# Merge gates of a hybrid decoder layer as seven block products each

## The chip, the cores and the metric

The kernel runs on one core of a Trainium2 chip. TensorE multiplies matrices into PSUM (8 banks of 128 x 512 fp32), VectorE, ScalarE and GpSimd work element by element, and DMA queues that SyncE issues move data between DRAM and SBUF. Each engine runs its own instructions strictly in the order in which they are written and meets the others through semaphores. The metric is the device time of one execution in microseconds. Every matrix product has fp32 accuracy by three passes: each operand is split into hi (ScalarE, a rounding copy) and lo (VectorE, the difference), and TensorE adds hi x hi, hi x lo and lo x hi.

## What is computed

One decoder layer: a half-step FFN, a token mixer with two branches, a half-step FFN. The part that matters here is the mixer, cut from the reference (1024 positions, model width 1024):

```python
u = _rmsnorm(h, mix_pre_g[l])
c_q, c_kv, k_rope_raw, xb, yb, gate_mla, gate_lru = jnp.split(u @ w_in[l], split_points, axis=-1)
o_mla = _mla_branch(c_q, c_kv, k_rope_raw, positions, ...)   # norms, up-projections, rotary, causal softmax, output projection
o_lru = _rglru_branch(xb, yb, conv_w[l], ...)                # below
merged = jax.nn.sigmoid(gate_mla) * o_mla + jax.nn.sigmoid(gate_lru) * o_lru
h = h + _rmsnorm(merged @ w_out[l], mix_post_g[l])

# _rglru_branch
xc = conv_b + sum(xpad[:, k:k + s] * conv_w[k] for k in range(CONV_WIDTH))
r  = jax.nn.sigmoid(einsum('bsgi,gij->bsgj', xg, w_rg) + b_rg)     # xg: xc in 8 blocks of 128
ig = jax.nn.sigmoid(einsum('bsgi,gij->bsgj', xg, w_ig) + b_ig)
a = jnp.exp(log_a);  gated_x = jnp.sqrt(-jnp.expm1(2.0 * log_a)) * (ig * xc)
_, h = lax.associative_scan(_lru_combine, (a, gated_x), axis=1)
return (h * jax.nn.gelu(yb)) @ w_o_lru
```

## The kernel before

Activations lie transposed, channels on partitions: `u_hi` and `u_lo` hold u as 8 chunks of 128 channels by 1024 positions. A projection of 128 output channels by all positions is 8 chunks x 2 halves x 3 passes = 48 matmuls of 512 columns. Weights come as blocks of 512 KB into a raw ring of three slots (`w.load` on SyncE, which waits until the block three before it is split); `w.hi` on ScalarE and `w.lo` on VectorE split them into a ring of three. The order of every engine's work is written out by hand.

The recurrence runs over 8 columns d of 128 channels. In round d TensorE does `gates_of(d)` (12 matmuls, recurrence and input gates from the convolved column), `y_of(d+1)` (48) and `x_of(d+2)` (48). VectorE convolves column d+1 out of PSUM (one tensor-scalar, three dependent multiply-adds), splits it, forms the factor under the root (`mix`), runs the scan (`scan`) and multiplies by the gelu branch (`gated`); between these it does the weight lo parts. ScalarE does the two sigmoids, the hi parts, two exponentials and a tanh (`decay`), the square root (`root`) and the next gelu; each change of function set is a table load. GpSimd multiplies twice per column (`products`). The finished column is split (`out_hi`, `out_lo`) into `lru_hi`, `lru_lo` in SBUF, where the branch projection reads it.

Then comes `LruMerge`: for each d, 48 matmuls of the gate (`gate_of`), whose sigmoid ScalarE takes out of PSUM, and 48 of the projection by w_o_lru (`branch_of`); VectorE multiplies both and the product goes to DRAM (`mixed_scratch`). After it `Latents`: eight tiles of 128 positions, `project` (48 matmuls of 384 or 288 columns), squares, scaling and transposes (`turn`), with one gate of the attention branch (`gate_of`, 48 matmuls) ahead of all but two of the projections, two of them ahead of the first; their sigmoids go to DRAM. Last, the value products (`v_of`) and the first units (`unit_of`) of attention, then the softmax steps; GpSimd clears six half-empty operand tiles (`blank`) before the first of them and divides each step's probabilities.

The two FFNs already use the block scheme that the change brings to the gates: a product of two 2 x 2 block matrices in seven block products instead of eight, with sums of blocks formed beforehand.

## Time and profile before

| | us |
|---|---|
| median of 3 runs | 2288.66 (2287.89 to 2289.98) |
| the profiled execution's own time | 2287.68 |
| its span, first to last instruction | 2285.9 |
| TensorE busy | 2154.8 (94%), 9837 matmuls |
| VectorE busy | 1387.9 (61%) |
| ScalarE busy | 975.1 (43%) |
| GpSimd busy | 450.0 (20%) |
| mean granted TensorE clock | 0.979 of full |

The span is cut by the profile into starts and durations of every instruction, in microseconds from its start. The listed duration of a matmul includes its way through the array; neighbours overlap, so what one costs is the distance between starts. The recurrence's rounds lie at 742 to 906, the gates and branch projection of `LruMerge` from there to 1080, the latents to 1231, attention's softmax steps from 1253 on.

### The profile page before, as it was taken

How to read it: one execution, taken by the hardware profiler on the slowest of the kernel's cores; microseconds unless marked ns; L12 is line 12 of the kernel's file. 1: busy time of each engine (PE TensorE's matmuls, PEld its weight loads, DVE VectorE, ACT ScalarE, POOL GpSimd, SP SyncE). 2: the span in 40 equal slices, each digit the busy share in tenths (PEclk: the TensorE clock that was granted, in tenths of full speed). 3: DMA queues.
4: the chain of work that ended last, by engine and by line, in shares of the span. 5: the costliest groups of instructions: out<-in, count | busy, mean ns of one | idle time of the engine just before them, and what ended most of it. 6: DMA issues, size and time to landing. Idle time of an engine off the chain costs nothing.

```text
span 2285.9 us, 25908 instructions
## 1 busy us (share of the span) xinstructions
PE 2154.8 (94%) x9837; PEld 1788.0 (78%) x9837; DVE 1387.9 (61%) x1718; ACT 975.1 (43%) x1543; POOL 450.0 (20%) x453
## 2 busy tenths in 40 slices
PE   4999999999998999999999888998599999999997
PEld 3888788878886888888888777777488888888885
DVE  7668865557575656211213788677756766557666
ACT  5333333334353776311323666445433333334343
POOL 5123320000032221000012555215312321000012
PEclk8999999999999999999999999999799999999998
DMA  3345442252442221222410100455135453216334
GB/s 120 93 155 187 155 168 69 70 198 96 154 148 78 52 52 49 74 65 77 119 43 23 29 15 10 161 194 175 55 96 188 168 192 124 72 51 221 101 134 143
DMA packets 220294, 249.85 MB, mean 109 GB/s; under 512 B 24262, under 2 KB 161547, under 8 KB 220171
## 3 DMA queue, kind: packets, MB, share of 16 engines
q1 hardware_dynamic: 220170, 248.19, 33.3%
q8 instruction: 79, 1.29, 0.2%
q14 instruction: 45, 0.36, 0.1%
HBM read 192.06 MB, written 55.57 MB: 108 GB/s over the span
## 4 chain that ended last, share of the span: by engine, by line
PE 86%; DVE 6%; ACT 3%; POOL 3%; issue 2%; DMA 1%; POOLq 0%; SPq 0%; ACTq 0%; DVEq 0%
PE ps L88 28%; PE ps L90 28%; PE ps L89 28%; PE ps L2172 1%; PE ps L2140 1%; POOL a_rot L2057 1%; PE ps L357 1%; ACT a_probs L2116 1%; DVE a_pt L98 1%; DVE ff_t L98 1%; DVE a_s L2106 0%; DVE entry_y L342 0%; DVE w_lo L98 0%; DMA w_raw<-in_w_out_dram 0%; ACT entry_squares L282 0%
## 5 line engine op out<-in xcount | busy, mean ns | idle before, releaser
L98 DVE TENSOR_TENSOR ff_w_lo<-ff_raw,ff_w_hi 128x512 fp32r<-128x512 f32 x264 | 210.9, 802 | 171.9 <-ACT ff_w_hi L94 171.7
L88 PE MATMUL ps<-ff_t,ff_w_hi 128*128 128x512 f32 x704 | 275.5, 391 | 15.8 <-DVE ff_t L98 15.8
L89 PE MATMUL ps<-ff_t,ff_w_hi 128*128 128x512 f32 x704 | 275.1, 391 | 0.0
L90 PE MATMUL ps<-ff_t,ff_w_lo 128*128 128x512 f32 x704 | 275.1, 391 | 0.0
L94 ACT ACTIVATE ff_w_hi<-ff_raw 128x512 fp32r<-128x512 f32 x264 | 164.8, 628 | 180.4 <-PE ps L90 174.9
L88 PE MATMUL ps<-d_b_hi,d_a_hi 128*128 128x512 f32 x608 | 237.6, 391 | 3.7 <-DVE d_a_lo L98 3.7
L98 DVE TENSOR_TENSOR w_lo<-w_raw,w_hi 128x1024 fp32r<-128x1024 f32 (+2 forms) x81 | 93.6, 1160 | 237.4 <-ACT w_hi L94 237.3
L90 PE MATMUL ps<-d_b_hi,d_a_lo 128*128 128x512 f32 x608 | 236.8, 390 | 0.0
L89 PE MATMUL ps<-d_b_lo,d_a_hi 128*128 128x512 f32 x608 | 236.8, 389 | 0.0
L88 PE MATMUL ps<-ff_b,ff_w_hi 128*128 128x512 f32 x528 | 209.0, 396 | 13.5 <-issue 8.3
L89 PE MATMUL ps<-ff_b,ff_w_hi 128*128 128x512 f32 x528 | 207.8, 394 | 0.0
L90 PE MATMUL ps<-ff_b,ff_w_lo 128*128 128x512 f32 x528 | 207.6, 393 | 0.0
L88 PE MATMUL ps<-u_hi,w_hi 128*128 128x512 f32 x512 | 201.0, 393 | 2.4 <-DVE u_lo L98 2.4
L89 PE MATMUL ps<-u_lo,w_hi 128*128 128x512 f32 x512 | 200.4, 391 | 0.0
L90 PE MATMUL ps<-u_hi,w_lo 128*128 128x512 f32 x512 | 200.4, 391 | 0.0
L88 PEld LDWEIGHTS ps<-ff_t,ff_w_hi 128*128 128x128 f32 x704 | 133.0, 189 | 44.0 <-issue 16.3
L89 PEld LDWEIGHTS ps<-ff_t,ff_w_hi 128*128 128x128 f32 x704 | 132.9, 189 | 27.6
L90 PEld LDWEIGHTS ps<-ff_t,ff_w_lo 128*128 128x128 f32 x704 | 132.8, 189 | 27.7
L94 ACT ACTIVATE w_hi<-w_raw 128x1024 fp32r<-128x1024 f32 (+2 forms) x81 | 78.1, 968 | 165.2 <-PE ps L90 155.0
L88 PEld LDWEIGHTS ps<-d_b_hi,d_a_hi 128*128 128x128 f32 x608 | 114.2, 188 | 28.9 <-DVE d_a_lo L98 5.7
L90 PEld LDWEIGHTS ps<-d_b_hi,d_a_lo 128*128 128x128 f32 x608 | 114.2, 188 | 23.8
L89 PEld LDWEIGHTS ps<-d_b_lo,d_a_hi 128*128 128x128 f32 x608 | 114.2, 188 | 23.5
(296 smaller groups left out, 4362.4 us busy)
## 6 DMA issues: line engine op xcount, KB each, us to landing
ff_raw<-in_ffn_w_gate_dram SPq DMA_DIRECT2D x44, 512.0 KB, 3.9
ff_raw<-in_ffn_w_up_dram SPq DMA_DIRECT2D x44, 512.0 KB, 4.0
d_sums<-in_ffn_w_down_dram SPq DMA_DIRECT2D x44, 512.0 KB, 4.1
sums_scratch<-d_sums SPq DMA_DIRECT2D x88, 256.0 KB, 2.6
w_raw<-in_w_in_dram SPq DMA_DIRECT2D x32, 512.0 KB, 3.9
d_raw<-sums_scratch SPq DMA_DIRECT2D x24, 512.0 KB, 3.3
w_raw<-in_w_out_dram SPq DMA_DIRECT2D x24, 512.0 KB, 4.3
spill_scratch<-ff_st SPq DMA_DIRECT2D x44, 256.0 KB, 2.6
```

The costliest lines, as they stand in the source:

```text
L88: pe.matmul(out, lh, rh, start=start, stop=False, skip_group_check=go_on)
L89: pe.matmul(out, lh, rl, start=False, stop=False, skip_group_check=go_on)
L90: return pe.matmul(out, ll, rh, start=False, stop=stop, skip_group_check=go_on)
L94: return nc.scalar.activation(hi, src, ACT.Copy)
L98: return nc.vector.tensor_tensor(lo, src, as_f32(hi), ALU.subtract)
L357: last = pe.transpose(self.c.ps[:, b + k // 4, (k % 4) * P:(k % 4 + 1) * P], self.work(t)[:, k * P:(k + 1) * P], self.c.ident[:, :])
L2057: self.nc.gpsimd.tensor_tensor(self.rot[rope, :], self.rot[rope, :], self.rot2[rope, :], ALU.add)\
L2116: self.nc.scalar.activation(self.prob(n), self.seen(n), ACT.Exp, bias=self.neg[:, i:i + 1], scale=1.0, accum_out=self.rs[:, i:i + 1]).then ...
L2140: last = pe.transpose(c.ps[:, 4 + b, at * P:(at + 1) * P], self.prob(n)[:, j * P:(j + 1) * P], c.ident[:, :])
L2172: last = pe.matmul(c.ps[:, 6, first * P:HALF], self.v[:, h, j, :], pt[:, unit, first:4, :].rearrange("p b q -> p (b q)"), start=j + i == 0 ...
```

## The change

Both gates are taken out of `LruMerge` and `Latents` and computed together by a new class, `MergeGates`, right after the recurrence. For each gate, w_gate^T u is a product of 2 x 2 blocks (halves of the channels, halves of the positions and of the inputs). A chunk m is one pair of 128-channel rows, one in each half; there are 8 chunks, 4 for each gate, and for each of them seven products p of 12 matmuls, 672 in all where there were 768. The sums of activation blocks (`t_wholes`, `t_sums`, `t_hi`, `t_lo`) are formed once, during the recurrence's rounds 1 to 5, the last one at its end; the sums of weight blocks (`sums`) per chunk. Three PSUM banks serve a chunk, and a product that continues in a bank waits until ScalarE has copied out the bank's state (`snap`); VectorE adds further banks (`cadd`) into the copy.

The space that `lru_hi` and `lru_lo` had holds the activation sums now. So a recurrence column is stored to DRAM unsplit (`keep`), and the next convolution into its buffer waits for that store. The columns are loaded and split again after the last latent projection (`row_hi`, `row_lo`) into the place of u, and the branch projection stands there, behind the latents; the gates' sigmoids all go to DRAM and those of this branch are loaded back for its products. The last column's projection is cut into its lo half and two hi halves, with the first attention units between them. The clearing of attention's tiles waits until the last product is stored.

The diff, cut:

```diff
+def gate_order():
+
+    order = [(0, 1), (0, 2), (0, 6), (0, 7), (0, 5)]
+    for m in range(1, G_CHUNKS):
+        order += [(m, 1), (m, 2), (m - 1, 3), (m - 1, 4), (m, 6), (m, 7), (m, 5)]
+    return order + [(G_CHUNKS - 1, 3), (G_CHUNKS - 1, 4)]
...
+    def product(self, pe, m, p):
+        c, F, S = self.c, self.c.f, self.rec.S
+        self.wait_split(pe, m, p)
+        if p == 1:
...
+            elif m == 0:
+                pe.wait_ge(S["conv_done"], DK)
+                pe.wait_ge(S["gelu_done"], DK)
...
+        if p == 6:
+            pe.wait_ge(F.snap[1], self.nm(m))
...
+        if p == 5:
+            pe.wait_ge(F.snap[6], self.nm(m))
...
+        for k in range(4):
+            lhs = tuple(x[:, slot, k * P:(k + 1) * P] for x in (self.hi_at, self.lo_at))
+            last = mm3(pe, out, lhs, self.right_of(p, k), k == 0 and p in (1, 2, 7), k == 3, p not in (1, 2, 7))
...
-    def out_hi(self, act, d):
...
+    def keep(self, sp, d):
+
+        sp.wait_ge(self.S["out_done"], d + 1)
+        sp.dma_start(self.kept[d * P:(d + 1) * P, :], self.xc[:, d % 2, :]).then_inc(self.c.f.d_in[2 + d % 2], 16)
...
     def convolve(self, dve, d):
         self.w.wait_done(dve, self.n_x[d])
         if d >= 2:
-            dve.wait_ge(self.S["out_split"], d - 1)
+            self.wait_kept(dve, d - 2)
...
     def blank(self, pool):
-        pool.wait_ge(self.lat.S["proj_done"], NT)
+        self.wait_unit(pool, self.units[0])
+        self.merge.all_stored(pool)
...
                     rec.mix(dve, d)
                     rec.scan(dve, d)
-                    if d + 2 <= DK:
-                        w.lo(dve, (rec.n_y + [ring[1]])[d + 2])
+                    if 1 <= d <= 4:
+                        gates.t_sums(dve, d - 1)
+                    if d + 2 < DK:
+                        w.lo(dve, rec.n_y[d + 2])
                     rec.gated(dve, d)
...
-                lru.gate_of(pe, 0)
-                lru.gate_of(pe, 1)
-                lru.branch_of(pe, 0, tuple(range(DK - 1)))
-                lru.branch_of(pe, 0, (DK - 1,))
...
+                for m, p in G_ORDER:
+                    gates.product(pe, m, p)
                 lat.project(pe, 0)
-                lat.project(pe, 1)
-                lat.turn(pe, 0)
-                for s in range(2, NT):
-                    lat.gate_of(pe, s)
+                for s in range(1, NT):
+                    lat.project(pe, s)
                     lat.turn(pe, s - 1)
-                    lat.project(pe, s)
-
-                att.v_of(pe, 0)
-                att.v_of(pe, 1)
+
+                for t in range(4):
+                    att.v_of(pe, t)
+                lat.turn(pe, NT - 1)
+                for k in range(DK):
+                    for d in range(2):
+                        lru.branch_of(pe, d, k)
+                    if k < 4:
+                        att.v_of(pe, k + 4)
+                for d in range(2, DK - 1):
+                    for k in range(DK):
+                        lru.branch_of(pe, d, k)
+                lru.last_lows(pe)
                 att.unit_of(pe, units[0])
...
+                lru.last_highs(pe, 0)
                 att.unit_of(pe, units[2])
-                att.v_of(pe, NT - 1)
+                lru.last_highs(pe, 1)
                 att.unit_of(pe, units[3])
```

What stands in a row on three engines, before and after. VectorE in a middle round of the recurrence, before, from the scan to the next convolution:

```order
L1499 SCALAR_TENSOR_TENSOR r_xc<-r_a,r_xc 128x1024 [waits r_bx_done]
L98 TENSOR_TENSOR w_lo<-w_raw,w_hi 128x1024 [waits w_hi_done]
L1505 TENSOR_TENSOR r_xc<-r_xc,r_gate_y_140 128x1024 [waits r_gelu_done,r_scan_done]
L98 TENSOR_TENSOR lru_lo<-r_xc,lru_hi 128x1024 [waits r_out_hi]
L98 TENSOR_TENSOR w_lo<-w_raw,w_hi 128x1024 [waits w_hi_done]
L1478 TENSOR_SCALAR r_xc<-ps,params 128x1024 [waits r_out_split,w_used]
```

After, from the scan of round 3 to the next convolution (`g_t_raw` is the activation sums' raw place, `g_t` their hi and lo parts):

```order
L1502 SCALAR_TENSOR_TENSOR r_xc<-r_a,r_xc 128x1024 [waits r_bx_done]
L1657 TENSOR_TENSOR g_t_raw<-g_t_raw 128x512 [waits g_t_sum]
L1658 TENSOR_TENSOR g_t_raw<-g_t_raw 128x512
L1660 TENSOR_TENSOR g_t_raw<-g_t_raw 128x512 [waits g_t_sum]
L1663 TENSOR_TENSOR g_t_raw<-g_t_raw 128x512 [waits g_t_sum]
L98 TENSOR_TENSOR w_lo<-w_raw,w_hi 128x1024 [waits w_hi_done]
L1508 TENSOR_TENSOR r_xc<-r_xc,r_gate_y_140 128x1024 [waits r_gelu_done,r_scan_done]
L98 TENSOR_TENSOR w_lo<-w_raw,w_hi 128x1024 [waits w_hi_done]
L98 TENSOR_TENSOR g_t<-g_t_raw,g_t 128x4x512 [waits g_t_hi]
L1641 TENSOR_TENSOR g_t_raw<-u_hi,u_lo 128x2x512
L1644 TENSOR_TENSOR g_t_raw<-u_hi,u_lo 128x2x512
L1481 TENSOR_SCALAR r_xc<-ps,params 128x1024 [waits d_in2,w_used]
```

The split of the finished column went out; four sums came between scan and weight split, and the split of an earlier set and two adds of whole operands between the last weight split and the convolution, which now waits for the store (`d_in2`).

ScalarE at the end of the recurrence (last column), before, from the first exponential to the first gate's sigmoid:

```order
L1452 ACTIVATE r_a<-r_r,rates 128x1024 [waits r_sig_r]
L1454 ACTIVATE r_b<-r_r,rates 128x1024 [waits r_ix_done]
L1457 ACTIVATE r_r<-r_r,rates 128x1024 [waits r_a2_done,r_a_done]
L1461 ACT_TABLE_LOAD
L1461 ACTIVATE r_r<-r_r 128x1024 [waits r_m_done]
L94 ACTIVATE lru_hi<-r_xc 128x1024 [waits r_out_done]
L94 ACTIVATE w_hi<-w_raw 128x1024 [waits w_used,w_raw_in1]
L1602 ACT_TABLE_LOAD [waits r_out_split]
L1602 ACTIVATE m_sig_149<-ps 128x1024 [waits w_used]
```

After, the same place (`g_w_hi` is the operand ring of the gates, `g_sig` the copies of banks):

```order
L1451 ACTIVATE r_a<-r_r,rates 128x1024 [waits r_sig_r]
L1453 ACTIVATE r_b<-r_r,rates 128x1024 [waits r_ix_done]
L1456 ACTIVATE r_r<-r_r,rates 128x1024 [waits r_a2_done,r_a_done]
L1460 ACT_TABLE_LOAD
L1460 ACTIVATE r_r<-r_r 128x1024 [waits r_m_done]
L1778 ACTIVATE g_sig_153<-ps 128x512 [waits r_out_done,f_prod]
L94 ACTIVATE g_w_hi<-g_s_151 128x512 [waits f_prod,f_sums]
L94 ACTIVATE g_w_hi<-w_raw 128x512 [waits f_prod,f_raw_in2]
L1796 ACT_TABLE_LOAD
L1796 ACTIVATE g_sig_153<-g_sig_153 128x512 [waits f_cadd2]
L1778 ACTIVATE g_sig_154<-ps 128x512 [waits f_prod]
```

Behind the root there now stands the copy of the first product's bank; the first sigmoid of a gate and the copy of the third product's bank follow it.

GpSimd at attention's start, before:

```order
L1967 MEMSET a_q_167 32x1024 [waits l_proj_done]
L1967 MEMSET a_q_169 32x1024
L1967 MEMSET a_k_171 32x1024
L1967 MEMSET a_k_174 32x1024
L1967 MEMSET a_k_172 32x1024
L1967 MEMSET a_k_175 32x1024
L2057 TENSOR_TENSOR a_rot<-a_rot,a_rot_178 32x512 [waits a_q_rot,a_zero]
L1752 TENSOR_TENSOR l_kr_t<-l_kr_t,trig 32x512 [waits l_c_split,l_rs_done,a_q_sum]
L1755 TENSOR_TENSOR l_rot<-l_rot,l_kr_t 32x512 [waits l_swapped,l_plain]
L2057 TENSOR_TENSOR a_rot<-a_rot,a_rot_178 32x512 [waits a_q_rot,l_rotated]
L2122 TENSOR_TENSOR a_s_184<-a_s_183,expo 128x1 [waits a_p_done,a_q_sum]
L2125 TENSOR_SCALAR a_probs<-a_probs,a_s_184 128x128 [waits a_norm_done]
```

After:

```order
L2375 TENSOR_TENSOR a_rot<-a_rot,a_rot_185 32x512 [waits a_q_rot,l_rotated]
L2375 TENSOR_TENSOR a_rot<-a_rot,a_rot_185 32x512 [waits a_q_rot,a_q_sum]
L2287 MEMSET a_q_174 32x1024 [waits m_stored0,m_stored1,a_unit_done,a_q_sum]
L2287 MEMSET a_q_176 32x1024
L2287 MEMSET a_k_178 32x1024
L2287 MEMSET a_k_181 32x1024
L2287 MEMSET a_k_179 32x1024
L2287 MEMSET a_k_182 32x1024
L2440 TENSOR_TENSOR a_s_191<-a_s_190,expo 128x1 [waits a_p_done,a_zero]
L2443 TENSOR_SCALAR a_probs<-a_probs,a_s_191 128x128 [waits a_norm_done]
```

The six clearings went behind the rotary sums and wait for the stores of the mixed products (`m_stored`) and the first unit; the first division of probabilities follows them as before.

## Rows read from the trace of the kernel before

**Rows 1.** Page, parts 1 and 4: busy time, and the chain that ended last.

```profile
PE 2154.8 (94%) x9837; PEld 1788.0 (78%) x9837; DVE 1387.9 (61%) x1718; ACT 975.1 (43%) x1543; POOL 450.0 (20%) x453
...
PE 86%; DVE 6%; ACT 3%; POOL 3%; issue 2%; DMA 1%; POOLq 0%; SPq 0%; ACTq 0%; DVEq 0%
```

**Rows 2.** Busy time by stretch.

```profile
core 0: us, PE busy (x) PEld busy (x) DVE busy (x) ACT busy (x) POOL busy (x), PEclk, DMA share, GB/s
735.00:906.00 171.00, 171.00 (x756) 141.69 (x755) 107.69 (x85) 121.74 (x115) 33.65 (x14) 1.00 0.19 48
1096.00:1231.00 135.00, 135.00 (x740) 122.23 (x739) 22.40 (x52) 39.71 (x115) 12.70 (x30) 1.00 0.21 59
1231.00:1260.00 29.00, 23.38 (x108) 18.18 (x106) 19.49 (x34) 17.31 (x39) 12.34 (x15) 1.00 0.04 9
```

**Rows 3.** TensorE timeline: start, duration, both in us, then line, operands, shape.

```profile
889.58 0.39 PE L88 MATMUL ps<-r_xc_hi,r_g_hi 128*128 128x512 f32 x1
...
905.90 0.39 PE L88 MATMUL ps<-u_hi,w_hi 128*128 128x512 f32 x1
```

**Rows 4.** VectorE timeline, one round of the recurrence.

```profile
792.03 1.34 DVE L1478 TENSOR_SCALAR r_xc<-ps,params 128x1024 f32<-128x1024 f32 x1
...
797.24 1.22 DVE L98 TENSOR_TENSOR r_g_lo<-r_raw_g,r_g_hi 128x256 fp32r<-128x256 f32 x1
...
808.05 2.29 DVE L1499 TENSOR_TENSOR_SCAN r_xc<-r_a,r_xc 128x1024 f32<-128x1024 f32 x1 [3.62 <-POOL r_xc L1519]
...
813.72 1.23 DVE L98 TENSOR_TENSOR lru_lo<-r_xc,lru_hi 128x1024 fp32r<-128x1024 f32 x1 [1.13 <-ACT lru_hi L94]
...
816.34 1.34 DVE L1478 TENSOR_SCALAR r_xc<-ps,params 128x1024 f32<-128x1024 f32 x1 [0.26 <-PE ps L90]
```

**Rows 5.** GpSimd, ScalarE and VectorE timelines, and tile a_o_lo: durations.

```profile
795.77 2.41 POOL L1516 TENSOR_TENSOR r_xc<-r_b,r_xc 128x1024 f32<-128x1024 f32 x1 [11.72 <-ACT r_b L1444]
...
740.64 2.00 ACT L94 ACTIVATE w_hi<-w_raw 128x1024 fp32r<-128x1024 f32 x2
...
741.72 2.36 DVE L98 TENSOR_TENSOR w_lo<-w_raw,w_hi 128x1024 fp32r<-128x1024 f32 x2 [2.06 <-ACT w_hi L94]
...
L98 DVE TENSOR_TENSOR a_o_lo<-a_o,a_v x2: 683/688/693, 1453.9 to 1468.4; 128x512 fp32r<-128x512 f32 x2
```

**Rows 6.** ScalarE and VectorE timelines, end of the recurrence.

```profile
912.40 1.28 ACT L1444 ACT_TABLE_LOAD   x1
...
921.88 1.06 ACT L1461 ACTIVATE r_r<-r_r 128x1024 f32<-128x1024 f32 x1
...
925.44 2.29 DVE L1499 TENSOR_TENSOR_SCAN r_xc<-r_a,r_xc 128x1024 f32<-128x1024 f32 x1 [3.61 <-POOL r_xc L1519]
```

**Rows 7.** TensorE timeline after a long idle, and busy time of that stretch.

```profile
57.06 0.77 PE L88 MATMUL ps<-ff_t,ff_w_hi 128*128 128x512 f32 x1 [15.78 <-DVE ff_t L98]
...
57.00:62.30 5.30, 5.24 (x13) 4.14 (x14) 5.27 (x8) 0.88 (x2) 1.04 (x1) 0.51 0.00 0
```

**Rows 8.** ScalarE and VectorE timelines around the latent projections.

```profile
1080.17 2.08 ACT L94 ACTIVATE l_w_hi<-w_raw 128x672 fp32r<-128x672 f32 x3 [9.76 <-PE ps L90]
...
1093.99 0.86 DVE L98 TENSOR_TENSOR l_w_lo<-w_raw,l_w_hi 128x672 fp32r<-128x672 f32 x1 [1.37 <-ACT l_w_hi L94]
...
1234.27 0.94 ACT L1716 ACTIVATE l_lat<-ps,l_s 128x384 f32<-128x384 f32 x2 [0.82 <-POOL l_s L1740]
...
1244.38 0.88 ACT L1725 ACTIVATE cq<-ps,params 128x128 fp32r<-128x128 f32 x3
```

**Rows 9.** TensorE and GpSimd timelines at attention's start, and a DMA issue.

```profile
1253.62 0.33 PE L88 MATMUL ps<-a_k,a_q 96*128 96x128 f32 x1 [0.94 <-DVE a_v L98]
...
1260.63 0.48 PE L2140 MATMUL ps<-ident,a_probs 128*128 128x128 f32 x1 [0.31 <-POOL a_probs L2125]
...
1235.97 3.62 POOL L1967 MEMSET a_k<- 32x1024 f32 x4
...
mixed_scratch<-m_prod SPq DMA_DIRECT2D x8, 512.0 KB, 3.7
```

707 lines of the change are left out of this document (483 added, 224 removed).

## The prediction, made before the changed kernel was timed

> **What bounds the kernel now.** I read three views in this order. The page's busy line and its chain that ended last say TensorE: 2154.8 us busy of 2285.9, 86% of the chain [rows 1]. An average over stages does not say what an edit is worth, so next comes the busy time by stretch: from 735 to 906 (recurrence) and from 1096 to 1231 (latents) TensorE has no gap at all, and only around 1231 to 1260 (entry to attention) does it lose 5.6 us [rows 2]. So in the stretches that the change rewrites, TensorE's queue is the time. A matmul of 512 columns costs its issue pace, not its listed 0.39 us: 12 + 48 + 12 matmuls lie between 889.58 and 905.90, 0.227 us each [rows 3]. Last I read VectorE, ScalarE and GpSimd in one round of the recurrence [rows 4, 5]. They are not the bound, but their round is one chain: the next convolution starts 816.34 - 792.03 = 24.3 us after the last, against TensorE's round of 108 matmuls, 24.5 us, and two microseconds of that go to waits for each other. Whoever adds work in line there has almost no room.
>
> **What it removes.** Gates: 768 matmuls become 672. 96 x 0.227 = **-21.8 us**, on the path, since TensorE never waits there. Branch projection, latents and attention keep their matmul counts. The 16 weight splits, 16 gate sigmoids and the split of the recurrence's result come back as 56 splits, 32 half-wide sigmoids, 24 copies, 24 adds, 32 sums: per block row some 9 to 10 us of VectorE at 0.69 each [rows 5] beside 84 matmuls (19 us). From the second block row on that stays hidden: a copied bank is asked for two or more products later (5.4 us), and the operand ring is four products deep. I take 0 for the steady state, 0 to +4 for the range.
>
> **What it adds in the recurrence.** In rounds 1 to 4 VectorE gets two whole-operand adds, four sums and a split of 2048 columns, ScalarE a split of 2048. The order puts the sums between scan and weight split, the split and the adds before the next convolution: all of it in line, none of it in the gaps where VectorE waits for ScalarE and GpSimd. A round from convolution to convolution: to the scan's end 18.3 (792.03 to 810.34) [rows 4]; sums 4 x 0.65 = 2.6; ScalarE's split of the sums, which stands ahead of the next weight's hi part, 2.0, that hi part 1.0, the lo part 1.15; the split's lo part 2.3; the adds 2 x 1.15 = 2.3 (1024 columns pace 1.15 on VectorE, 1.0 on ScalarE) [rows 5]. Sum 29.7 against TensorE's 24.5. The pair of splits it saves (2.3 with its wait of 1.13) is already out of that sum. Starts: round 1 at 768.1 as before (what it gains, the first adds take); then 797.8, 827.5, 856.8 (the fourth set has one block less), 882.5 (only three sums, no further adds). Round 6 has only two half-wide splits, but its convolution now waits until the buffer it overwrites has been stored: gated product 1.2, then a store that lands in some 3.2 us (the same size took 3.7 on median [rows 9]; this buffer's twin in the latents stage was quicker). 906.4, where before stood 889.8: 16.6 late.
> TensorE absorbs part. Its round d needs the weight split that now stands behind the sums, and convolution d+1 before it may overwrite its bank; going through rounds 3 to 5 with these starts it waits 3.0, 4.8 and 2.5 us. Its last recurrence matmuls need the convolved column split at 906.4 + 7.7 = 914.1 and end at 916.8 instead of 905.9: **+10.9** (bounds 6 and 16).
> A rule that bears on this: the row of 797.24 shows a 256-column split on VectorE stretched to 1.22 us; it ended 0.28 us after GpSimd's product (795.77 + 2.41), while the convolution, which reads PSUM, ran through beside that product undisturbed [rows 4, 5]. The Trainium skill (SBUF — State Buffer, section SBUF: two separate sides) says that a VectorE instruction with two SBUF inputs and a GpSimd instruction that reads SBUF exclude each other for the whole instruction. The new adds and split have two SBUF inputs; by the rule they would sit out part of GpSimd's product. In the new round GpSimd's product would start about 26.3 us after the convolution (sums split 22.9, hi part 1.0, table load 1.3, sigmoid 1.1), just ahead of the adds at 27.4: up to 1.6 us more in each of three rounds. I count it as a rival.
>
> **What it does at the seam.** Before, 24 us of other matmuls (two gates, most of a projection) ran while the last column's sigmoids, exponentials, root and scan finished; ScalarE's root ended at 922.94, 17 us after TensorE was done with the recurrence, and nobody waited [rows 3, 6]. Now the first product waits for the last gelu, and the third waits for ScalarE's copy of the first one's bank, which stands behind that root. Counted from the last convolution's start C: scan 18.3, gated 1.2, four sums 2.7, two hi parts 1.2 on ScalarE, then table load to root 10.5 (912.40 to 922.94) [rows 6], copy 0.6: C + 34.5 = 940.9. Gelu: root 13.5, table load and gelu 2.4, so C + 15.9 = 922.3, **+5.5**. Two products take 5.4, then TensorE stands **13.2** us until 940.9. The fifth product waits for the copy of the third's bank, behind a sigmoid that waits for VectorE's add, which stands behind scan and gated product (2.4 + 2.3 + 1.2 + 0.7 + 0.6 + 0.6 after the root): **+2.0**. Seam: +20.7; even without any delay from the rounds it would be 12.8 + 2.0. After an idle of 15.78 us the granted clock read 0.51, its 1.2 GHz level, for 5.2 us, so 12 matmuls took 0.43 us each, 2.4 more in all [rows 7]; here the first ones after 940.9 would be as slow, and the wait of 2.0 swallows most: **+0.4** (0 to 5).
>
> **What it does in the latents and after.** No gates are left to lie between the projections. (a) The first projection wants eight split weights. The raw ring holds three; each later one costs a load of 3.5 us after a split, and the eight took from 1080.17 to 1094.85 [rows 8], hidden then by 21.8 us of gates. Now only two products (5.4 us) and the projection's own 7.6 cover them, and VectorE's last bank add stands among the splits: **+3.7** with the last chunk's exposed copy (2 to 7). (b) Behind the last projection ScalarE has some 7.5 us queued (squares, columns 1.5, scaling 0.94, two row copies of 1.0, two half-wide ones) [rows 5, 8] while TensorE has 4.8 of transposes and value products: **+3.3** (0 to 6). The rows read back from DRAM start three deep and are eaten at 2.7 to 4.1 us each: hidden. The five later projections, 10.9 us each, cover their weights and gate loads: 0. (c) Units of attention now alternate with the last column's halves, which covers TensorE's waits before 1253.62, some 3.4 of the 5.6: -3.4. But GpSimd's six clearings (5.4 us) [rows 9], before already begun at 1234, now wait until the last product has been stored, and the first softmax's division waits behind them: product 4.4 us after the last unit, store 3.7, clearings 5.5, against 6.3 us before: +7.4, of which short early steps catch up some 2. Net **+2** (-3 to +7).
>
> **Sum**, against the profiled execution's own 2287.7 (span 2285.9 plus 1.8 around it; the median is 2288.7): -21.8 + 10.9 + 20.7 + 0.4 + 3.7 + 3.3 + 2 = +19.2: **2307**.
>
> **Rivals.** (1) The shared port holds the adds back: three rounds of 1.6 more, 2312. For it, the 797.24 row; against, the late order may move GpSimd's product clear of them. (2) Slack absorbs the recurrence: if VectorE's new work costs nothing in line (its busy time would be only some 23 of 24.5 us), just the seam's 14.8 stays: -21.8 + 14.8 + 0.4 + 7 + 2 = +2.4, 2290, no change. Against it, every one of those instructions stands in one queue with the waits of [rows 4]. (3) **Faster**, the other side: the chain at the seam does not reach TensorE. Its place is the third product; it decides if the first bank's copy is free before 911.4, which takes a root ending 12 us earlier than 922.94; then -21.8 + 7 + 2 = 2275. The row speaks against it. (4) Worse after the recurrence: clock at 1.2 GHz after several of the short waits, the first attention steps recovering nothing, weights late: +5, +5 and +3 on the forecast, 2320. (5) That it doesn't do what it says (fewer matmuls issued) is excluded by the order, which has 672.
>
> **Chances.** Forecast 0.45, rival 1 0.17, rival 4 0.17, rival 2 0.11, rival 3 0.10. A measurement of this kernel tells about 0.2%, 4.6 us, from no change. Slower: forecast, 1 and 4, 0.79. Same: 0.11. Faster: 0.10. The range leaves rival 3 and the far end of 4 out: **2289 to 2320**.
>
> **What would show it.** Right: 96 matmuls less; TensorE idle in 790 to 900 before weights' lo parts and convolutions, about 10 us, then one wait of about 13 us before a block product, ended by ScalarE's copy, with a dip of the granted clock; one wait before the first latent projection; GpSimd's clearings after the last store. VectorE's round some 29 to 31 us long in rounds 1 to 3. Wrong: rounds still of 24.5 us, or a third product that starts at once; then the time falls to rival 2 or 3. If block rows in the steady state show gaps, the 0 for them is wrong.

## The result, and the profile after

The changed kernel takes 2315.97 us (median of 4 runs, 2314.51 to 2316.95) beside 2288.69 of the kernel before (2287.89 to 2289.98): ratio 1.0118, 95% interval 1.0101 to 1.0136. It is **slower by 27 us**, where 2307 was forecast and the range ended at 2320. Measured a second time, without an edit, it took 2320.39 (2317.37 to 2323.96; 2289.41 for the kernel before beside it): 31 us, and just past the end of the range.

The page, parts 1 and 4: busy time, and the chain that ended last.

```profile
PE 2143.5 (93%) x9741; PEld 1773.9 (77%) x9741; DVE 1473.1 (64%) x1845; ACT 1012.4 (44%) x1628; POOL 454.4 (20%) x453
...
PE 78%; DVE 8%; issue 6%; POOL 3%; ACT 3%; DMA 1%; POOLq 0%; SPq 0%; ACTq 0%; DVEq 0%
```

The 96 matmuls are gone (9837 to 9741), and TensorE's part of the chain fell from 86% [rows 1] to 78%: more of the chain now runs through other engines and waits. Where they lie is shown by the busy time by stretch. The columns are as in [rows 2]. The cuts are TensorE's starts: recurrence, from there to product 1 of block row 1 (the seam), steady block rows, value products, first scores. A block row is what the code calls a chunk m, and product p of block row m is written (m,p); the products up to (1,1) are the first five.

```profile
737.92:919.94 182.02, 168.59 (x721) 136.63 (x719) 125.06 (x102) 111.70 (x104) 33.22 (x13) 0.98 0.22 63
919.94:954.60 34.66, 18.13 (x63) 14.14 (x62) 18.45 (x21) 22.42 (x25) 7.05 (x3) 0.75 0.08 31
954.60:1094.38 139.78, 139.00 (x614) 114.82 (x613) 66.45 (x101) 57.23 (x102) 0.00 (x0) 1.00 0.36 110
...
1161.54:1172.55 11.01, 8.02 (x34) 6.24 (x32) 7.16 (x12) 7.45 (x20) 1.45 (x4) 0.85 0.36 107
1271.93:1290.00 18.07, 7.12 (x27) 5.32 (x26) 8.06 (x13) 6.12 (x12) 7.78 (x11) 0.73 0.35 84
```

Before, TensorE had no gap from 735 to 906 [rows 2]; now it is idle for 13.4 us of the recurrence and 16.5 of the seam, and in the seam the granted clock is 0.75. The steady block rows are as full as forecast. Some of the longest waits, from TensorE's timeline (start, duration, line, operands; in brackets the idle time ahead and who ended it):

```profile
817.55 0.50 PE L88 MATMUL ps<-u_hi,w_hi 128*128 128x512 f32 x1 [2.71 <-DVE w_lo L98]
832.55 0.47 PE L88 MATMUL ps<-u_hi,w_hi 128*128 128x512 f32 x1 [3.81 <-DVE r_xc L1486]
...
925.45 0.76 PE L88 MATMUL ps<-u_hi,g_w_hi 128*128 128x512 f32 x1 [5.25 <-ACT r_gate_y L1435]
943.94 0.76 PE L88 MATMUL ps<-g_t,g_w_hi 128*128 128x512 f32 x1 [11.27 <-issue]
...
1167.54 0.80 PE L88 MATMUL ps<-w_hi,ckv 128*128 128x512 f32 x1 [2.99 <-DVE a_v L98]
...
1276.72 0.57 PE L88 MATMUL ps<-a_k,a_q 96*128 96x256 f32 x1 [4.26 <-DVE m_sig L1939]
1288.40 0.47 PE L2458 MATMUL ps<-ident,a_probs 128*128 128x128 f32 x1 [6.69 <-POOL a_probs L2443]
```

The first pair is one round of the recurrence, in which a weight's lo part and a convolution come late. VectorE's and GpSimd's timelines of that round answer to [rows 4, 5]:

```profile
820.42 2.28 DVE L98 TENSOR_TENSOR g_t<-g_t_raw,g_t 128x2048 fp32r<-128x2048 f32 x1
822.63 3.42 DVE L1641 TENSOR_TENSOR g_t_raw<-u_hi,u_lo 128x1024 f32<-128x1024 f32 x1
825.98 1.21 DVE L1644 TENSOR_TENSOR g_t_raw<-u_hi,u_lo 128x1024 f32<-128x1024 f32 x1
827.11 1.33 DVE L1481 TENSOR_SCALAR r_xc<-ps,params 128x1024 f32<-128x1024 f32 x1
...
821.76 3.21 POOL L1514 TENSOR_TENSOR r_xc<-r_b,r_xc 128x1024 f32<-128x1024 f32 x1 [10.24 <-ACT r_b L1443]
```

Two adds of the same size and shape take 3.42 and 1.21 us. The first meets GpSimd's product, which itself takes 3.21 us and not the 2.41 of [rows 5]. The convolution before this one had started at 795.54, so the round took 31.6 us, where 29.7 was forecast and 24.5 is what TensorE needs. The next two took 31.0 and 26.6 (29.3 and 25.7 forecast).

At the seam, ScalarE's timeline holds the root, and right behind it the copy for which the third product waits. TensorE's row at 943.94 names no releaser (`issue`); that it is this copy follows from the code, where this product waits for `snap[1]`, and from the copy's end at 943.84. At attention's entry GpSimd's clearings wait for the last store:

```profile
942.30 1.06 ACT L1460 ACTIVATE r_r<-r_r 128x1024 f32<-128x1024 f32 x1
943.26 0.58 ACT L1778 ACTIVATE g_sig<-ps 128x512 f32<-128x512 f32 x1
...
1281.85 1.83 POOL L2287 MEMSET a_q<- 32x1024 f32 x2 [11.86 <-DMA mixed_scratch<-m_sig]
1283.62 3.62 POOL L2287 MEMSET a_k<- 32x1024 f32 x4
```

### The profile page after: what moved, and what is told of

Same layout as the page of the kernel before. It is cut to its first block, busy times and chain, and to the rows that moved or that the text cites. A ratio compares the mean times of both kernels' runs of the same rounds, so it can differ in the third digit from the quotient of the medians.

```text
span 2315.2 us, 26065 instructions
## 1 busy us (share of the span) xinstructions
PE 2143.5 (93%) x9741; PEld 1773.9 (77%) x9741; DVE 1473.1 (64%) x1845; ACT 1012.4 (44%) x1628; POOL 454.4 (20%) x453
## 4 chain that ended last, share of the span: by engine, by line
PE 78%; DVE 8%; issue 6%; POOL 3%; ACT 3%; DMA 1%; POOLq 0%; SPq 0%; ACTq 0%; DVEq 0%
PE ps L88 25%; PE ps L89 25%; PE ps L90 25%; PE ps L2490 1%; PE ps L2458 1%; PE ps L357 1%; POOL a_rot L2375 1%; ACT a_probs L2434 1%; DMA w_raw<-in_w_out_dram 1%; DVE a_pt L98 1%; DVE w_lo L98 1%; DVE a_s L2424 0%; DVE ff_t L98 0%; POOL r_xc L1514 0%; POOL r_xc L1517 0%
## 5 line engine op out<-in xcount | busy, mean ns | idle before, releaser
L98 DVE TENSOR_TENSOR ff_w_lo<-ff_raw,ff_w_hi 128x512 fp32r<-128x512 f32 x264 | 216.2, 823 | 171.5 <-ACT ff_w_hi L94 171.3
L98 DVE TENSOR_TENSOR w_lo<-w_raw,w_hi 128x1024 fp32r<-128x1024 f32 (+2 forms) x65 | 73.9, 1142 | 90.4 <-ACT w_hi L94 90.4
L88 PEld LDWEIGHTS ps<-ff_b,ff_w_hi 128*128 128x128 f32 x528 | 100.4, 190 | 35.6 <-issue 14.9
L90 PEld LDWEIGHTS ps<-ff_b,ff_w_lo 128*128 128x128 f32 x528 | 100.2, 190 | 21.1
L89 PEld LDWEIGHTS ps<-ff_b,ff_w_hi 128*128 128x128 f32 x528 | 100.3, 190 | 20.7
L88 PE MATMUL ps<-u_hi,w_hi 128*128 128x512 f32 x256 | 102.2, 399 | 14.1 <-DVE r_xc L1486 7.4
```

The source lines that it names most:

```text
L88: pe.matmul(out, lh, rh, start=start, stop=False, skip_group_check=go_on)
L89: pe.matmul(out, lh, rl, start=False, stop=False, skip_group_check=go_on)
L90: return pe.matmul(out, ll, rh, start=False, stop=stop, skip_group_check=go_on)
L98: return nc.vector.tensor_tensor(lo, src, as_f32(hi), ALU.subtract)
```

## The experiments

All kernels but the first are the changed one with the edit shown; the code is cut and shortened. The table cuts the span of each profile at the same TensorE starts (us): until the recurrence's first gate matmul; recurrence; seam, to product (1,1); from there to the first latent projection; value products, to the first branch matmul; first score to first transpose; and from there to the end. What is not shown (latents 66.5 to 68.2, branch projection 99.4) hardly differs. Where the last gate matmuls of the recurrence come late, the first wait of the seam is shorter by as much, for both hang on the same last column: the sum of recurrence and seam is steadier (216.1 to 217.2 us in the six profiles in which neither was edited) than either of them.

| kernel | until | recurrence | seam | block rows | values | entry | rest | median |
|---|---|---|---|---|---|---|---|---|
| before | 742.7 | 163.2 | | | | 7.0 | 1025.3 | 2288.7 |
| changed | 737.9 | 182.1 | 34.6 | 139.8 | 11.0 | 16.5 | 1026.8 | 2316.0 |
| after_again | 741.6 | 183.9 | 32.6 | 139.8 | 12.3 | 14.1 | 1031.3 | 2320.4 |
| e1_gaps | 739.9 | 163.5 | 34.1 | 139.8 | 10.8 | 14.1 | 1029.0 | 2297.2 |
| e2_poollate | 739.7 | 175.3 | 34.6 | 139.8 | 11.0 | 14.1 | 1029.8 | 2312.6 |
| e3_seam | 739.8 | 182.0 | 34.0 | 139.8 | 11.0 | 14.1 | 1027.0 | 2319.7 |
| e4_entry | 742.8 | 181.7 | 34.4 | 139.8 | 11.0 | 6.5 | 1027.0 | 2311.2 |
| e5_seam2 | 742.7 | 183.7 | 22.5 | 143.9 | 11.0 | 14.1 | 1029.6 | 2313.4 |
| e6_all | 737.8 | 164.0 | 22.8 | 143.8 | 9.8 | 6.5 | 1027.4 | 2283.4 |
| e7_prod7 | 739.9 | 183.6 | 33.5 | 139.8 | 11.0 | 9.4 | 1028.1 | 2311.5 |
| e8_values | 740.2 | 183.5 | 33.7 | 139.8 | 8.2 | 14.1 | 1027.8 | 2316.5 |
| e9_all2 | 741.2 | 164.2 | 23.1 | 146.4 | 8.2 | 6.5 | 1029.6 | 2285.7 |
| e10_clear | 742.7 | 182.4 | 34.5 | 139.8 | 11.0 | 9.6 | 1030.9 | 2317.7 |
| e11_last | 739.9 | 163.7 | 23.3 | 141.8 | 8.2 | 6.5 | 1027.4 | 2280.0 |

**The changed kernel again.** No edit.

> The changed kernel once more, beside the other three on the same chip: 2316 (2313 to 2319). In the six profiles so far the recurrence's first gate matmul starts between 737.92 and 742.84 us although nothing ahead of it differs between the kernels; if that is chance, this profile lies in the same band, and the 4.8 us by which the changed kernel seemed ahead there mean nothing; if the change itself made the stretch ahead of it faster, it is 738 again.

Until the first gate 741.6, inside the band of 737.8 to 742.8 that all the profiles make, in which the kernel before lies too. So the 4.8 us by which the first profile of the changed kernel was ahead there are chance. The median was not 2316 again but 2320.39, above the 2313 to 2319 that I had expected: the loss against before is 27 us in one set of runs and 31 in the other. Medians of these kernels carry some 2 us of such scatter each way; the stretches of one profile are the sharper measure.

**The recurrence, order.** In VectorE's round:

```
-  if 1 <= d <= 4: gates.t_wholes(dve, d - 1)
   rec.convolve(dve, d + 1); rec.gates_lo(dve, d + 1); rec.conv_lo(dve, d + 1)
+  if 1 <= d <= 4: gates.t_wholes(dve, d - 1)
   rec.mix(dve, d)
+  if 1 <= d <= 4: gates.t_sums(dve, d - 1)
   rec.scan(dve, d)
-  if 1 <= d <= 4: gates.t_sums(dve, d - 1)
```

> The changed kernel with two of VectorE's three new pieces moved inside the round of the recurrence: the whole-operand adds from ahead of the next convolution to behind its split (where VectorE stood 3.5 us idle before the mix), the four sums from behind the scan to between mix and scan (3.6 us idle there). Same instructions, same count. Theory A (they cost because they stand in line in one round of work): the line gets shorter by 3.4 + 1.2 + 2.7 = 7.3 us in rounds of 31.6, which falls under TensorE's 24.5; the recurrence goes from 182.0 back to 163 to 167 us, the kernel from 2316 to about 2299 (2297 to 2304). Rival B (TensorE waits in these rounds for something else, the store of the kept column for one): less than 3 us gained, 2313 or more, and the same idle rows before the weights' lo parts and convolutions. The seam behind the recurrence keeps its 34.7 us by both.

2297.22 us (2297 to 2304 expected; ratio to before 1.0037, 1.0022 to 1.0052); recurrence 163.5, TensorE busy in all but 0.1 us of it. VectorE's timeline of a round, with GpSimd's second product:

```profile
816.94 1.34 DVE L1481 TENSOR_SCALAR r_xc<-ps,params 128x1024 f32<-128x1024 f32 x1 [0.88 <-DMA kept_scratch<-r_xc]
...
824.51 1.22 DVE L1641 TENSOR_TENSOR g_t_raw<-u_hi,u_lo 128x1024 f32<-128x1024 f32 x1
825.64 1.22 DVE L1644 TENSOR_TENSOR g_t_raw<-u_hi,u_lo 128x1024 f32<-128x1024 f32 x1
...
831.19 2.77 DVE L1663 TENSOR_TENSOR g_t_raw<-g_t_raw 128x512 f32<-128x512 f32 x1
...
830.54 2.87 POOL L1517 TENSOR_TENSOR r_xc<-r_xc,r_r 128x1024 f32<-128x1024 f32 x1 [10.72 <-ACT r_r L1460]
```

Theory A holds: the same instructions in the same number cost nothing once they stand where VectorE was idle. The convolution still waits 0.88 us for the store, and TensorE does not miss it. The collision is there too, now as a sum of 2.77 us for 0.69. But the scan waits for GpSimd's product anyway: it starts at 833.88, where the product, had it taken its 2.40 us, would have ended at 832.94, and TensorE does not miss that either.

**The recurrence, collision.** One wait more, on GpSimd:

```
   pool.wait_ge(self.S["xc_split"], d + 1)
+  if d + 1 < DK:
+      pool.wait_ge(self.S["conv"], (CONV - 1) * (d + 1) + 1)
   self.nc.gpsimd.tensor_tensor(to, self.b[:, :], to, ALU.mult)
```

> The changed kernel with one wait more on GpSimd: its first product of a round (2.4 us, two operands in SBUF) starts only when VectorE's next convolution has written its first tap, so that it lies beside the taps and no longer beside the whole-operand adds and splits; its reader comes 7 us later. No work is changed or moved on any other engine. Port theory (the two engines hold each other up, which took the first add from 1.22 to 3.42 us and the product from 2.40 to 3.21): all adds 1.2 us, the product 2.4, rounds of 29.4 for 31.6 us, the recurrence 5 to 6.6 us shorter, the kernel at 2310 (2309 to 2312). Queue theory (the adds take their time for another reason, and the round is the sum of what stands in line): the add stays at 3.4, rounds 31.6, the kernel within 1 us of 2316.

The same stretch of VectorE, and GpSimd's product, now behind the convolution's start:

```profile
822.09 1.22 DVE L1643 TENSOR_TENSOR g_t_raw<-u_hi,u_lo 128x1024 f32<-128x1024 f32 x1
823.23 1.22 DVE L1646 TENSOR_TENSOR g_t_raw<-u_hi,u_lo 128x1024 f32<-128x1024 f32 x1
824.36 1.34 DVE L1481 TENSOR_SCALAR r_xc<-ps,params 128x1024 f32<-128x1024 f32 x1
...
825.87 2.41 POOL L1516 TENSOR_TENSOR r_xc<-r_b,r_xc 128x1024 f32<-128x1024 f32 x1 [14.89 <-DVE r_xc L1481]
...
904.40 1.34 DVE L1481 TENSOR_SCALAR r_xc<-ps,params 128x1024 f32<-128x1024 f32 x1 [3.03 <-DMA kept_scratch<-r_xc]
```

Both adds take 1.22 us, the product 2.41 beside the taps, and the convolutions of two rounds lie at 795.01 and 824.36: 29.4 us. The recurrence is 6.8 us shorter than in the changed kernel, by an edit that only makes an engine wait. The port theory holds by the trace; the kernel's 2312.60 us lies 0.6 above its range and 3.4 below the changed kernel's first median. What is left over before, 175.3 - 163.2 = 12.1 us, is the price of standing in line, the store in the last row included: there the convolution starts 4.2 us after the gated product it waits for.

**The seam, first order.** ScalarE: last sigmoids ahead of the splits, first copy ahead of the root, second behind it; TensorE's wait for the gelu moved to the fourth product:

```
+  rec.sigmoids(act, d)
   gates.hi(act, 0, 6); gates.hi(act, 0, 7)
-  rec.sigmoids(act, d)
+  gates.snap(act, 0, 1)
   rec.decay(act, d); rec.root(act, d)
+  gates.snap(act, 0, 6)
```

> The changed kernel with the order at the seam changed on ScalarE: the last column's sigmoids ahead of the two weight splits of block row 0 that wait for VectorE's sums, the copy of the first product's bank behind those splits and so ahead of the last exponentials and the root, the copy of the third product's bank straight behind the root; and TensorE's first block product no longer waits for the last gelu, which the fourth one now does. Theory A (the wait at the seam is the place of the first copy behind the root): TensorE's first product starts at once, the third waits until about 933 instead of 943.9, then the fifth for the copy behind a root that ends some 3.5 us earlier: from the end of the last recurrence gates to the start of (1,1) 24 us instead of 34.7, the kernel about 2305 (2303 to 2308). Rival B (the seam is nested: behind each wait stands another, here the split of the last column's own sums for the ninth product, which needs scan and gated product): most of it comes back at that ninth product, 4 to 5 us gained, 2311.

2319.70 us (2305 forecast), the seam 34.0 for 34.6: nothing gained. TensorE's and VectorE's timelines:

```profile
937.15 0.76 PE L88 MATMUL ps<-g_t,g_w_hi 128*128 128x512 f32 x1 [9.82 <-DVE g_w_lo L98]
951.44 0.79 PE L88 MATMUL ps<-g_t,g_w_hi 128*128 128x512 f32 x1 [6.81 <-DVE g_w_lo L98]
...
932.67 2.71 DVE L1758 TENSOR_TENSOR w_raw<-w_raw 128x512 f32<-128x512 f32 x1
...
950.70 0.68 DVE L98 TENSOR_TENSOR g_w_lo<-g_s,g_w_hi 128x512 fp32r<-128x512 f32 x1
```

The first product starts at once and the third at 937.15, 15.4 us after the recurrence's last gates (23.9 in the changed kernel, 13 by theory A), but the fifth now waits until 951.44 for its weight's lo part, which VectorE makes at 950.70 behind scan, gated product and an add. Nor did the root come 3.5 us earlier: it ends 33.0 us after the start of the last convolution, for 33.9 in the changed kernel, for the two splits put ahead of the exponentials wait for VectorE's sums, one of which met GpSimd's product (2.71 us for 0.69). Rival B is right that the seam is nested, but named the wrong nested wait, and less came out than its 4 to 5 us.

**The seam, second order.** Sums of block row 0 into the gap ahead of the scan of the seventh column, four weights' hi parts into ScalarE's idle time ahead of the last sigmoids, their lo parts ahead of the last mix, both copies ahead of the root:

```
 ScalarE  hi 06, 07, 05, 11 | sigmoids | snap 1 | decay | snap 6 | root | hi 12, 03
 VectorE  mix(6) | sums(0) | scan(6) | gated(6) | lo 06, 07, 05, 11 | add | mix(7) | lo 12 | scan(7) | lo 03
```

> The changed kernel with the seam's work interleaved further, after the order of e3_seam gave nothing: VectorE's sums of block row 0 in its idle time between mix and scan of the seventh column; ScalarE's splits of the products (0,6), (0,7), (0,5), (1,1) in its idle time ahead of the last sigmoids; the first bank's copy behind the sigmoids, the third product's copy ahead of the root; the splits' lo parts ahead of the last mix, one ahead and one behind the last scan. Same instructions. Theory A (seam = a nest of waits, each of which has to go): third product at about 12 us after the last recurrence gates, fifth at 18.6, (1,1) at 21.3 (20 to 24) for 34.7, and the ninth product waits under 3 us for the last column's sums; kernel at 2304 (2302 to 2307). Rival B (behind these stands yet another wait, or the splits now beside GpSimd's product hold the scan up): (1,1) at 25 or later, or over 4 us idle before the ninth product, kernel above 2308.

The seam is 22.5 us (forecast 21.3), but 4.1 us come back in the block rows (143.9 for 139.8). Against the 34.6 of the first profile that would be 8.0 us net; but recurrence and seam together are 206.2 us for 216.7, so it is rather 10.5 - 4.1 = 6.4. The medians, measured side by side, say 7.0: 2313.35 for 2320.39 (2304 forecast; above 2308 was rival B). Both theories were partly right. The waits left are the third product's and, at the eighth, one of 2.22 us for ScalarE's copy, which stands behind the split of the last column's own sums; that product then took 4.4 us for 2.7, most of it at the 1.2 GHz level. And a split that was put beside GpSimd's product pays for that place (2.47 us for 0.69):

```profile
938.06 0.77 PE L88 MATMUL ps<-g_t,g_w_hi 128*128 128x512 f32 x1 [5.78 <-issue]
956.82 0.47 PE L88 MATMUL ps<-u_hi,g_w_hi 128*128 128x512 f32 x1 [2.22 <-ACT g_sig L1778]
...
947.08 2.47 DVE L98 TENSOR_TENSOR g_w_lo<-w_raw,g_w_hi 128x512 fp32r<-128x512 f32 x1 [3.12 <-ACT g_w_hi L94]
...
946.60 2.39 POOL L1517 TENSOR_TENSOR r_xc<-r_xc,r_r 128x1024 f32<-128x1024 f32 x1 [7.35 <-ACT r_r L1460]
```

**Entry of attention, both edits, then each alone.**

```
 (a) GpSimd, blank():   four clearings without self.merge.all_stored(pool);
                        the two of k_hi[2], k_lo[2] with it, behind pool_step(5)
 (b) VectorE:  att.unit_dve(units[2]) | lru.product(7) | att.unit_dve(units[3]) | ...
```

> The changed kernel with two edits at the entry of attention: of GpSimd's six clearings four are done without a wait for the last store, and the two that lie in the stored buffer come behind the sixth softmax step; and VectorE's last gate product stands ahead of the last unit's splits, not behind the key's split. Theory A (both waits of TensorE there, 4.26 and 6.69 us, are paid in full): from the first score to the first transpose 7 us as in the kernel before, instead of 16.5; the kernel 9.5 us faster, 2306.5 (2305 to 2309). Rival B (the early softmax steps catch the delay up, as I forecast 2 us of): 4 to 7 us gained, 2309 to 2312. Rival C: the two clearings moved behind hold up a division of a later step and give 2 us back.

> The changed kernel with one of the two edits of e4_entry alone: VectorE's last gate product directly behind the second query unit's work, ahead of the last unit's splits; GpSimd's clearings wait for its store as before. Theory A (one chain: late product, late store, late clearings): product 4.7 us earlier, so clearings too, and from the first score to the first transpose 11.8 us for 16.5, kernel 2311 (2310 to 2313). Rival B (two chains, the clearings late for their own reasons): only the wait of the second score goes, the first transpose stays at 16 us and more, and the kernel at 2316.

> The other of the two edits of e4_entry alone: four of GpSimd's six clearings without a wait for the last store, two behind the sixth softmax step; VectorE's last gate product stays where it is. From the first score to the first transpose the changed kernel takes 14.1 us in most profiles, with both edits 6.5, with the earlier product alone 9.4. If the two losses simply add (the late product costs its own wait of 4.3 us before the second score, the clearings the rest), this one takes 10.5 to 11.3 us, for the wait of the second score stays. If the clearings alone were the loss, it takes 7 us; if the late product alone, 13 us and more.

From first score to first transpose: both edits 6.5 us (2311.21), (b) alone 9.4 (2311.48), (a) alone 9.6 (2317.68, no gain beyond the scatter of the runs), against 14.1 in most profiles and 16.5 in the first one, in which the last store took 5.0 us to land. GpSimd's first clearing with (b) alone, TensorE's second score with (a) alone, its first transpose with both:

```profile
1276.89 1.83 POOL L2287 MEMSET a_q<- 32x1024 f32 x2 [4.79 <-DMA mixed_scratch<-m_sig]
...
1281.38 0.42 PE L88 MATMUL ps<-a_k,a_q 96*128 96x256 f32 x1 [4.26 <-DVE m_sig L1939]
...
1282.30 0.33 PE L2462 MATMUL ps<-ident,a_probs 128*128 128x128 f32 x1 [0.24 <-POOL a_probs L2447]
```

Of e7's theories A holds: the product 4.7 us earlier made store, clearings and transpose 4.7 earlier, one chain. Taken alone the two edits gain 4.7 and 4.5, together 7.6: nearly a sum, so neither loss is the whole; they share 1.6 us of their way. For (a) alone none of the three forecasts was right (10.5 to 11.3, 7, or 13 and more). Of e4's three, A has it in kind but not in size: I had put the gain at 9.5 from the one profile with the late store; against the usual 14.1 it is 7.6. Its time, 2311.21, lies in the range of rival B, but what B says is not in the trace. TensorE's forty-first row of transposes starts 125.4 and 125.8 us after the first in the two profiles of the changed kernel and 125.5 with both edits: the steps do not catch up, and the two late clearings cost nothing that shows (C falls). Kernels without any edit here also took up to 128.0 us for that stretch, and the one with (a) alone 128.6, so a cost of 2 us or less could hide in it.

**Value products.** The copies and splits of products 0 and 1 and the last scaling ahead of the first two row copies:

```
-  row_hi(0) | v_hi(0) | row_hi(1) | scale(7) | v_hi(1) | row_hi(2) | v_hi(2)
+  v_hi(0) | scale(7) | v_hi(1) | row_hi(0) | row_hi(1) | v_hi(2) | row_hi(2)
```

> The changed kernel with the order of ScalarE and VectorE behind the last latent projection changed: the copies and splits of the first two value products and the last scaling ahead of the first two row copies of the branch operand, which TensorE needs only later. From the first value product to the first branch matmul the changed kernel takes 11.0 us (in five of six profiles) for some 6 us of matmuls: 2.99 us idle for the first product's split, the rest a granted clock at its 1.2 GHz level and the last transpose. Theory A (the queue behind the projection, as forecast, is half of it): the idle before the third product falls to about 1.6, and the stretch to 8.5 to 9.6 us. Rival B (the other half is the clock that falls with any such wait, and it stays): the idle falls but the stretch stays above 10. The kernel's time moves by 1 to 2.5 us, which is at the edge of what these runs can tell; the trace decides.

The stretch is 8.2 us for 11.0, better than either theory had it. TensorE's third product, and the stretch with its clock in the last columns but two:

```profile
1170.11 0.50 PE L88 MATMUL ps<-w_hi,ckv 128*128 128x512 f32 x1 [1.74 <-DVE a_v L98]
...
1165.36:1173.59 8.23, 6.49 (x34) 5.04 (x32) 5.90 (x12) 7.47 (x20) 1.45 (x4) 1.00 0.10 21
```

The wait is 1.25 us shorter, and the other 1.5 came from the clock: the mean grant over the stretch was 0.85 (in the second profile 0.72, and 12.3 us), and now it is 1.00. Rival B is half right: the other half was the clock, but it does not stay with any wait. Nor does it fall with every wait of 2.98 us: e6_all, below, has that wait with a grant of 1.00, and 9.8 us.

```profile
1135.27:1145.07 9.80, 6.76 (x34) 4.96 (x32) 7.06 (x12) 7.45 (x20) 1.45 (x4) 1.00 0.32 102
```

The kernel's own time, 2316.52, does not show the gain beyond its scatter.

**All together, and twice more.**

> The changed kernel with the edits of e1_gaps, e5_seam2 and e4_entry together. Theory A (three separate losses): -18.6 in the recurrence, -13 at the seam, -10 at the entry of attention, together 2316 - 41.6 = 2274 (2270 to 2279), below the kernel before (2288.5) by some 14 of the 21.8 us that the missing matmuls are worth. Rival B (the losses overlap, or one hands its time to the next): 2282 or more.

2283.43 us (8 runs, ratio 0.9974, 0.9964 to 0.9984), where 2274 was forecast and 2282 or more was rival B. Yet each stretch is what it was alone: 164.0, 22.8 and 143.8, 6.5. The three losses are separate; but my -41.6 took the seam and the entry at more than they gave alone. With what the traces show, recurrence and seam taken together, it is -19.1 (e1_gaps: 197.6 for 216.7) - 6.4 (e5_seam2) - 7.6 = -33.1. From the mean of the two medians, 2318.2, that is 2285.1.

> The kernel of e6_all with what its trace still showed: at the seam the copy of the fifth product's bank ahead of ScalarE's split of the last column's own sums (TensorE waited 2.4 us for it), VectorE's split for the ninth product ahead of the sums of block row 1 (1.1 us and the products behind), and the order of e8_values. Theory A: from (1,1) to the first latent projection 140.0 to 141.5 us for 143.8, the value stretch 1 us shorter, kernel 2279 (2276 to 2282) beside 2283.4. Rival B (the waits move on once more, to the split of the last column's sums or the sums of block row 1): under 1.5 us gained at the seam, kernel 2281 to 2284.

2285.67 (11 runs, ratio 0.9983, 0.9974 to 0.9992), above both forecasts. Values 8.2 as hoped, but the block rows 146.4 for 143.8. Rival B in kind, and at an instruction that I had not looked at: by putting the split and the sums of block row 1 forward I left VectorE's add of the fourth bank behind them. The last experiment moves that one add into the 0.7 us in which VectorE waits for ScalarE:

```
   self.t_last(dve)
+  self.cadd(dve, 0, 7)
   self.t_last_lo(dve)
   self.lo(dve, 0, 4)
   self.sums(dve, 1)
```

> The kernel of e9_all2 with one instruction moved: VectorE's add of the fourth product's bank, for which the ninth product then waited 3.73 us because it stood behind the sums of block row 1, into the 0.7 us in which VectorE waits for ScalarE's split of the last column's sums. Theory A: the ninth product waits under 1 us, the tenth up to 1.3 us for its own weights' sums, and from (1,1) to the first latent projection 141.5 to 143 us for 146.4 (e6_all: 143.8); the kernel 2281 (2279 to 2284), below e6_all by less than the runs can tell. Rival B (the loss moves on in full to the tenth product, since VectorE's queue there is simply too long): 145 us and more, kernel 2285.

TensorE's ninth product in e9_all2, and the ninth and tenth in e11_last:

```profile
940.57 0.76 PE L88 MATMUL ps<-g_t,g_w_hi 128*128 128x512 f32 x1 [3.73 <-DVE g_sig L1786]
...
935.62 0.50 PE L88 MATMUL ps<-g_t,g_w_hi 128*128 128x512 f32 x1 [0.42 <-DVE g_w_lo L98]
939.67 0.50 PE L88 MATMUL ps<-g_t,g_w_hi 128*128 128x512 f32 x1 [1.01 <-DVE g_w_lo L98]
```

Block rows 141.8 (141.5 to 143 expected), 2279.97 us (10 runs, 2277.16 to 2284.34), **ratio to the kernel before 0.9967, 0.9957 to 0.9977**. So the change was worth making: the same work in another order takes 8.4 us less than the kernel before (2288.40 beside it), where as it stood it took 27 to 31 more. Of the 21.8 that the matmuls are worth the rest still goes to the seam (23.3 for five products of 13.6: 9.7), to the block rows (141.8 for 612 matmuls of 138.7: 3.1) and to the latents and values.

## Why the prediction was right, and where it was off

Direction and range held (the second median, 2320.39, ends 0.4 past the range); the time was 9 us too low (13 by the second measurement).

- **Matmuls, -21.8**: as forecast. TensorE waits nowhere in what they stood in.
- **Recurrence, +10.9**: measured +18.9. The step that failed is the price per round. I had the collision of adds and GpSimd's product in hand, from [rows 4, 5] and the rule named there, and made it a rival with 0.17, because "the late order may move GpSimd's product clear of them". I had computed the product's start myself, 1.1 us ahead of the adds, and then argued on no row that it might move. It was also undersized: 1.6 us a round, where the first add lost 2.2, and so did each of three rounds (31.6 us for 29.4 in e2_poollate). In the sixth round two weight splits met the product too (3.49 us for 1.29), but that cost nothing: the convolution behind them waited for its store in any case. Without the collision (e2_poollate) the rest is 12.1 us and the round 29.4 for my 29.7, so the sum over the line was right. Most of what 10.9 lacks of 12.1 is the store in the sixth round, 4.2 us from gated product to convolution where I had 3.2. Rival 2, that slack absorbs it, fell with the result, and e1_gaps shows why: slack absorbs the work only if it stands in the slack.
- **Seam, +20.7 + 0.4**: measured 34.66 - 13.6 = +21.1. Counted from the last convolution's start, ScalarE's copy ends after 34.4 us (forecast 34.5). By its parts: gelu 919.94 to 925.45, 5.5 for 5.5; two products and the wait 18.5 for 18.6; the last three products 10.7 us for 8.2, +2.5 where I had 2.0 of wait and 0.4 of clock. This last is right by luck: the slow clock alone (the third product took 5.2 us for 2.7) took the time in which I had the fifth product wait. The wait of the third product itself was 11.27 us for my 13.2, because the two products ahead of it ran in part at the lower clock (7.2 us for 5.4); as its end hangs on ScalarE's copy, that cost nothing. That the place was rightly read did not make it the only one: in e3_seam the third product started 8.5 us earlier and nothing came back. I had named three waits there; below them lay a fourth, a weight split behind scan and gated product.
- **Steady block rows, 0**: 139.8 for 138.7. Of the 1.1 us 0.78 is the last block row's copy, which I had counted in the next term; +0.3 is left.
- **First latent projection, +3.7**: as forecast. The latents take 67.2 us; before, the stretch from 905.90 to 1231.26 without the 261.1 us of its 1152 gate and branch matmuls leaves 64.2. That is +2.9, 2.3 of it in three waits of 0.7 to 0.8 us for weights' lo parts, and +0.8 with the copy makes 3.7.
- **Value products, +3.3**: +5.0 (+6.3 in the second profile). The wait was right (2.99); the clock that fell with it, 1.5 us (2.9 in the second), was not in the term.
- **Entry, +2**: +3.0 in most profiles, +5.4 in the first. Units between the last products saved 4.1 (3.4 forecast); the clearings cost 7.1 (7.4), 9.5 in the first profile. What failed is the 2 us that short early steps should catch up: nothing was caught up. The chain's first link, the product some 4.4 us behind the last unit, stood in the sum at about its size, but I took it as given; it was only VectorE's order, and e7_prod7 got 4.7 us back by it.
- **Together**, for the profiled execution: -4.8 ahead of any changed line, -21.8 + 18.9 + 21.1 + 1.1 + 2.9 + 5.0 + 5.4, and +1.5 behind the first transpose, make +29.3, which is 2316.95 - 2287.68. The first and the last of these no term had. The stretch behind the first transpose took 1025.3 us before and 1026.8 to 1031.3 in the kernels after, whatever their edit; whether its 1.5 us or more are the change's or chance, no run settles.

Rival 1 was the one that came true in its mechanism, with the clock of rival 4 at two places; rival 3 fell at its own point, the root that ended 23 us after the last recurrence gates.

## What to carry to other kernels

In a round that two or three engines share, work does not cost its busy time but its place: look for where the engine waits for others and put it there, and look what the neighbour does at that moment, since a VectorE instruction with two SBUF operands and a GpSimd product excluded each other here (3.42 us for 1.22). A wait at a seam is a nest; before moving one instruction, write down for each of the next matrix products which instruction it waits for and what stands ahead of that, on every engine, or the gain stops at the next one. And where one's own working gives a collision a time and a place, count it; it is a rival only if a row speaks against it.
